# Prompt attention scores in two rounded passes, and the samples' block scores sample by sample

## The reference

```python
s_c = jnp.einsum('btgrd,bngd->bgrtn', q, kc).astype(jnp.float32) * scale - slopes[:, :, None, None] * dist_c
p_c = masked_softmax(s_c, dist_c >= 0, (-1,))
o_cmp = jnp.einsum('bgrtn,bngd->btgrd', p_c, vc.astype(jnp.float32))
...
ss = jnp.einsum('qgrd,gqkld->grqkl', qb, kg).astype(jnp.float32) * scale - slopes[:, :, None, None, None] * dist[:, None]
pp = masked_softmax(ss, (dist >= 0)[:, None], (-2, -1))
...
ss = jnp.einsum('bqgrd,bkgd->bgrqk', qb, kv[:, :, 0]).astype(jnp.float32) * scale - slopes[:, :, None, None] * dist.astype(jnp.float32)
o = gates[..., 0:1] * o_cmp + gates[..., 1:2] * o_slc + gates[..., 2:3] * o_win
```

## Time and profile before

| | us |
|---|---|
| median of 3 runs | 4044.45 |
| runs | 4039.71 to 4048.02 |
| the profiled execution's own time | 4041.04 |
| its span in the profile | 4039.4 |
| the four rounds of the prompt's attention, first product with block keys to last transposes | 230.0 to 647.3 |
| fetch of the samples' blocks | 1018 to 1109 |
| TensorE busy over the span | 3489.2 (86%) |
| mean granted TensorE clock | 0.914 of full |

### The profile page before, as it was taken

The page is one execution under the profiler, slowest core; times in us unless marked ns, Lnnn a source line. Parts: engine busy times, 40 slices in busy tenths (PEclk is TensorE's granted clock), DMA queues, the critical chain, the costliest instruction groups (busy, mean ns, idle before and its releaser), DMA issues. The chain is left out here.

```text
span 4039.4 us, 64008 instructions
## 1 busy us (share of the span) xinstructions
PE 3489.2 (86%) x22287; PEld 3282.6 (81%) x22287; DVE 1353.9 (34%) x2028; ACT 1344.8 (33%) x2211; POOL 1483.8 (37%) x964
## 2 busy tenths in 40 slices
PE   5988887898088888799999998798997899999997
PEld 4966665898058777799999997788886799999997
DVE  3034442001003445443343332043345344343342
ACT  2134442000003443244344442233323244344442
POOL 2300001332403222246666664122222256666663
PEclk8978887899569999899999999899999899999998
DMA  1400001785200001134444443101111134444443
GB/s 71 129 17 0 0 0 48 258 266 164 78 11 32 32 32 58 59 99 139 137 138 149 144 151 106 48 28 39 51 38 54 58 114 133 138 140 133 143 137 124
DMA packets 158153, 372.99 MB, mean 92 GB/s; under 512 B 22410, under 2 KB 78026, under 8 KB 156316
## 3 DMA queue, kind: packets, MB, share of 16 engines
q1 hardware_dynamic: 116828, 310.96, 23.9%
q10 hardware_dynamic: 29440, 32.78, 2.5%
q0 software_dynamic: 11776, 27.80, 2.1%
HBM read 352.76 MB, written 22.89 MB: 93 GB/s over the span
## 5 line engine op out<-in xcount | busy, mean ns | idle before, releaser
L493 POOL TENSOR_TENSOR back_WL<-back_RAW,back_WH 128x1024 fp32r<-128x1024 f32 (+1 forms) x408 | 956.1, 2350 | 679.3 <-ACT back_WH L594 678.2
L532 PE MATMUL PS<-back_TH,back_WH 128*128 128x344 f32 x2112 | 676.9, 321 | 13.9 <-DVE back_TL L703 13.9
L532 PE MATMUL PS<-back_TL,back_WH 128*128 128x344 f32 x2112 | 674.7, 319 | 0.0
L532 PE MATMUL PS<-back_TH,back_WL 128*128 128x344 f32 x2112 | 674.4, 319 | 0.0
L594 ACT ACTIVATE back_WH<-back_RAW 128x1024 fp32r<-128x1024 f32 (+1 forms) x408 | 421.6, 1033 | 523.2 <-DMA back_RAW<-in_w 350.7
L532 PEld LDWEIGHTS PS<-back_TH,back_WH 128*128 128x128 f32 x2112 | 397.9, 188 | 15.6 <-issue 15.6
L532 PEld LDWEIGHTS PS<-back_TL,back_WH 128*128 128x128 f32 x2112 | 398.0, 188 | 0.0
L532 PEld LDWEIGHTS PS<-back_TH,back_WL 128*128 128x128 f32 x2112 | 397.8, 188 | 0.0
L741 DVE TENSOR_TENSOR back_HL<-back_TMP,back_HH 128x344 f32 x132 | 323.1, 2447 | 126.5 <-ACT back_HH L607 126.5
L1076 PE MATMUL PS<-layer_XH,layer_WH 128*128 128x344 f32 x960 | 325.9, 339 | 32.8 <-POOL layer_WL L1026 28.5
L532 PE MATMUL PS<-back_HH,back_WH 128*128 128x344 f32 x1056 | 338.4, 320 | 0.0
(11 more groups left out here) (365 smaller groups left out, 6079.3 us busy)
## 6 DMA issues: line engine op xcount, KB each, us to landing
back_RAW<-in_w SPq DMA_DIRECT2D x360, 512.0 KB, 3.3
layer_AR<-in_cmp SPq DMA_DIRECT2D x192, 128.0 KB, 4.3
layer_AR<-in_cmp POOLq DMA_DIRECT2D x192, 128.0 KB, 4.1
back_RAW<-in_w SPq DMA_DIRECT2D x48, 384.0 KB, 3.1
layer_AR<-in_cmp ACTq DMA_DIRECT2D x128, 128.0 KB, 4.1
layer_WR<-in_w_even SPq DMA_DIRECT2D x54, 256.0 KB, 2.8
layer_WR<-in_w_odd SPq DMA_DIRECT2D x50, 256.0 KB, 2.9
XT<-in_xT SPq DMA_DIRECT2D x4, 1032.0 KB, 7.8
```

The source lines that it names most:

```text
L493: pool.tensor_tensor(lo, raw, hi.bitcast(F32), ALU.subtract).then_inc(wl_ready, 1)
L532: mm = pe.matmul(m.PS[:, bank, 0:CH], wgt[:, t % RING, w], tok[:, k0 + k], start=(k0 + k + n == 0), stop=(last and n == 2 and k == kt - 1))
```

## The change

**Prompt scores.** The queries are now split: `m.QS` has, for group g, the query rounded to fp32r in g's own 64 rows (ScalarE, as before) and the remainder, rounded too, in the other 64 rows that were zero (VectorE, a new subtraction in each round for each group). The keys are doubled over both row halves and rounded (`m.KHD`, one tensor for each kind and group, in the place of tiles that are no longer needed), and their remainders stand in `m.KL`. One scores product becomes two fp32r products into the same PSUM region: `QS` (128 rows) by `KHD` (high query and low query by high key), then the 64 rows of the high query by `KL`. The block keys likewise become `KCH` and `KCL`, both over 128 rows. The splits are made at the start of the stage: kind 0's rounding on ScalarE (four copies of 64x1024) and its remainders on VectorE, kind 1's both on GpSimd (four products by one and two subtractions, 64x1024 each), the block keys' on VectorE. The large memset of `m.QP` goes.

**Samples.** The fetch loops are unrolled over the eight samples, each sample has its own two semaphores, and TensorE goes through the products sample by sample: it waits for that sample's blocks, and does for each group the first row half and then the second.

```diff
@@ attention_memory
-    m.QP = carve(m.AR, r, (G, SEQ))
+    m.QS = nc.alloc_sbuf_tensor_at("att_QS", [P, G, SEQ], F32R, offset=m.at_ar + 4 * r)
+    m.KHD = [[nc.alloc_sbuf_tensor_at(f"att_KHD{kind}{g}", [P, SEQ], F32R, offset=m.at_ar + 4 * TOK * tile)
+              for g, tile in enumerate(tiles)] for kind, tiles in enumerate(((TKC, TVC), (TVS, TVW)))]
+    m.KL = [nc.alloc_sbuf_tensor_at(f"att_KL{kind}", [P, SEQ], F32R, offset=m.at_ar + 4 * TOK * tile)
+            for kind, tile in enumerate((TKS, TKW))]
...
@@ attention
-        zeroed = m.dve.n + 2
+        zeroed = m.dve.n + 1
+        halves = [slice(g * DH, (g + 1) * DH) for g in range(G)]
...
+        @block.gpsimd
+        def _(pool):
+            for g in range(G):
+                for half in (halves[g], halves[1 - g]):
+                    pool.tensor_tensor(m.KHD[1][g][half], NT[halves[g], TKW, 0:SEQ],
+                                       m.ones[halves[g], 0:1].to_broadcast([DH, SEQ]), ALU.mult).then_inc(kx_ready, 1)
+            pool.wait_ge(kx_ready, 4 + ONE)
+            for half, high in zip(halves, m.KHD[1]):
+                pool.tensor_tensor(m.KL[1][half], NT[half, TKW, 0:SEQ], high[half].bitcast(F32), ALU.subtract)\
+                    .then_inc(kx_ready, 1)
...
+                    if s == 0:
+                        pe.wait_ge(kl_ready, 2 + ONE)
+                    elif s == QT:
+                        pe.wait_ge(kx_ready, 6 + ONE)
+                    half = halves[g]
                     for a in range(k0, k1, 512):
                         b = min(a + 512, k1)
-                        mm = pe.matmul(sbank(s)[:, a - k0:b - k0], m.QP[:, g, i * P:(i + 1) * P],
-                                       NT[:, TKS if kind == 0 else TKW, a:b], start=True, stop=True)
+                        pe.matmul(sbank(s)[:, a - k0:b - k0], m.QS[:, g, i * P:(i + 1) * P], m.KHD[kind][g][:, a:b],
+                                  start=True, stop=False)
+                        mm = pe.matmul(sbank(s)[:, a - k0:b - k0], m.QS[half, g, i * P:(i + 1) * P],
+                                       m.KL[kind][half, a:b], start=False, stop=True)
...
-                pe.wait_ge(q_ready, (r + 1) * 2 + ONE)
+                pe.wait_ge(kc_ready, 8 + ONE)
+                pe.wait_ge(ql_ready, (r + 1) * 2 + ONE)
...
-                        mm = pe.matmul(m.PS[:, 7, c0:c0 + PBLK], m.QP[:, g, i * P:(i + 1) * P], m.KCT,
-                                       start=True, stop=True)
+                        pe.matmul(m.PS[:, 7, c0:c0 + PBLK], m.QS[:, g, i * P:(i + 1) * P], m.KCH[:, g],
+                                  start=True, stop=False)
+                        mm = pe.matmul(m.PS[:, 7, c0:c0 + PBLK], m.QS[:, g, i * P:(i + 1) * P], m.KCL[:, g],
+                                       start=False, stop=True)
...
         @block.scalar
         def _(act):
+            for g in range(G):
+                act.activation(m.KHD[0][g][halves[g]], NT[halves[g], TKS, 0:SEQ], ACT.Copy).then_inc(kh_ready, 1)
+            for g in range(G):
+                act.activation(m.KHD[0][g][halves[1 - g]], NT[halves[g], TKS, 0:SEQ], ACT.Copy).then_inc(kh_ready, 1)
...
             t = m.dve
-            t.up(dve.memset(m.QP, 0.0))
             t.up(dve.memset(m.PC, 0.0))
+            for g in range(G):
+                for half in (halves[g], halves[1 - g]):
+                    dve.tensor_copy(m.KCH[half, g], m.KCT[halves[g]]).then_inc(kc_ready, 1)
...
+            dve.wait_ge(kh_ready, 4 + ONE)
+            for half, high in zip(halves, m.KHD[0]):
+                dve.tensor_tensor(m.KL[0][half], NT[half, TKS, 0:SEQ], high[half].bitcast(F32), ALU.subtract)\
+                   .then_inc(kl_ready, 1)
...
+                    dve.wait_ge(q_ready, r * 2 + g + 1 + ONE)
+                    dve.tensor_tensor(m.QS[halves[1 - g], g:g + 1], NT[halves[g], ds(r, 1), 0:SEQ],
+                                      m.QS[halves[g], g:g + 1].bitcast(F32), ALU.subtract).then_inc(ql_ready, 1)
@@ sample_select
-            with eng.Fori(0, NB) as b:
+            for b in range(NB):
...
-            pe.wait_ge(blocks_in, 20 * NB * 16)
-            pe.wait_ge(pool_in, 10 * NB * 16)
             pe.wait_ge(idx_ready, 2)
-            for half in range(2):
-                rows = slice(half * DH, (half + 1) * DH)
-                for n in range(NBG16):
+            for n in range(NBG16):
+                if n % G == 0:
+                    pe.wait_ge(blocks_in[n // G], 20 * 16)
+                    pe.wait_ge(pool_in[n // G], 10 * 16)
+                for half in range(2):
+                    rows = slice(half * DH, (half + 1) * DH)
                     mm = pe.matmul(m.PS[0:ROWS, 2 + half, :].rearrange("p (a b) -> p a b", b=BLK),
```

More of the change, by code:

```diff
@@ L1509, in _, with attention_memory @@
             closing(HEADS - 1, False)
-def attention_memory(m):
+def attention_memory(nc, m):
     W = m.WR
@@ L1527, in attention_memory @@
     m.HC = carve(m.AR, r + 4352, (2, G * PBLK), 0, DH)
-    m.QP = carve(m.AR, r, (G, SEQ))
+    m.QS = nc.alloc_sbuf_tensor_at("att_QS", [P, G, SEQ], F32R, offset=m.at_ar + 4 * r)
[3 more added lines that the diff above has]
+            for kind, tile in enumerate((TKS, TKW))]
+    at_kc = m.at_ar + 4 * (r + 6144)
+    m.KCH = nc.alloc_sbuf_tensor_at("att_KCH", [P, G, PBLK], F32R, offset=at_kc)
+    m.KCL = nc.alloc_sbuf_tensor_at("att_KCL", [P, G, PBLK], F32R, offset=at_kc + 4 * G * PBLK)
     m.AS = carve(m.LC, 0, (G, SEQ))
@@ L1664, in attention @@
         q_ready = sem("q_ready")
+        ql_ready = sem("ql_ready")
+        kh_ready, kl_ready = sem("kh_ready"), sem("kl_ready")
+        kx_ready, kc_ready = sem("kx_ready"), sem("kc_ready")
         bias_ready = sem("bias_ready")
@@ L1759, in _ @@
         def _(act):
+            for g in range(G):
+                act.activation(m.KHD[0][g][halves[g]], NT[halves[g], TKS, 0:SEQ], ACT.Copy).then_inc(kh_ready, 1)
+            for g in range(G):
+                act.activation(m.KHD[0][g][halves[1 - g]], NT[halves[g], TKS, 0:SEQ], ACT.Copy).then_inc(kh_ready, 1)
             with act.Fori(0, R) as r:
-                act.wait_ge(m.dve.sem, zeroed)
                 act.wait_ge(qk_ready, r * NS + ONE)
                 for g in range(G):
-                    half = slice(g * DH, (g + 1) * DH)
-                    act.activation(m.QP[half, g:g + 1], NT[half, ds(r, 1), 0:SEQ], ACT.Copy).then_inc(q_ready, 1)
+                    act.activation(m.QS[halves[g], g:g + 1], NT[halves[g], ds(r, 1), 0:SEQ], ACT.Copy)\
+                       .then_inc(q_ready, 1)
                 act.wait_ge(cp_step, r * 9 + 3 + ONE)
@@ L1798, in _ @@
             t = m.dve
-            t.up(dve.memset(m.QP, 0.0))
             t.up(dve.memset(m.PC, 0.0))
+            for g in range(G):
+                for half in (halves[g], halves[1 - g]):
+                    dve.tensor_copy(m.KCH[half, g], m.KCT[halves[g]]).then_inc(kc_ready, 1)
+            dve.wait_ge(kc_ready, 4 + ONE)
+            for g in range(G):
+                for half in (halves[g], halves[1 - g]):
+                    dve.tensor_tensor(m.KCL[half, g], m.KCT[halves[g]], m.KCH[halves[g], g].bitcast(F32), ALU.subtract)\
+                       .then_inc(kc_ready, 1)
+            dve.wait_ge(kh_ready, 4 + ONE)
+            for half, high in zip(halves, m.KHD[0]):
+                dve.tensor_tensor(m.KL[0][half], NT[half, TKS, 0:SEQ], high[half].bitcast(F32), ALU.subtract)\
+                   .then_inc(kl_ready, 1)
             dve.wait_ge(t.sem, zeroed)
@@ L2236, in sample_select @@
         idx_ready = sem("idx_ready")
-        blocks_in = sem("blocks_in")
-        pool_in = sem("pool_in")
+        blocks_in = [sem(f"blocks_in{b}") for b in range(NB)]
+        pool_in = [sem(f"pool_in{b}") for b in range(NB)]
         ss_ready, ss_neg, se_ready = sem("ss_ready"), sem("ss_neg"), sem("se_ready")
@@ L2248, in fetch @@
             eng.wait_ge(idx_ready, 1)
-            with eng.Fori(0, NB) as b:
+            for b in range(NB):
                 for n in range(0, len(slots), 4):
                     some = slots[n:n + 4]
-                    rows = [eng.value_load(m.IDX[0:1, ds(b * (G * TOPK) + slot, 1)]) for slot in some]
+                    rows = [eng.value_load(m.IDX[0:1, b * (G * TOPK) + slot:b * (G * TOPK) + slot + 1]) for slot in some]
                     for slot, row in zip(some, rows):
@@ L2255, in fetch @@
                         half = slice(s % 2 * DH, s % 2 * DH + DH)
-                        eng.dma_start(m.KVG[half, ds(b, 1), g, s // 2], d["slc"][ds(row, 1), g]
+                        eng.dma_start(m.KVG[half, b:b + 1, g, s // 2], d["slc"][ds(row, 1), g]
                                       .rearrange("n p c -> p n c"))\
-                            .then_inc(pool_in if eng is nc.gpsimd else blocks_in, 16)
+                            .then_inc((pool_in if eng is nc.gpsimd else blocks_in)[b], 16)
         @block.sync
@@ L2427, in program @@
             with mixer_memory(nc, m, "layer0"):
```

(2 more changed lines are left out.)

## The result

The changed kernel takes 4192.92 us (median of 4 runs, 4181.94 to 4248.02) against 4045.13 of the kernel before: a ratio of 1.0358, 95% interval 1.0319 to 1.0397. The ratio leaves out the run of 4248.02, which lies 1.6% above the fastest. The change makes the kernel slower by 3.6%, inside the forecast's range and on its side, but 83 us under its number.

A forecast was written before the change was run, and what follows sets the result against it. TensorE bounds the prompt attention's steps, and the samples' fetch and products are exposed. From 4041.04 us, 248 + 11.5 + 18 - 36 - 7 = +234.5 gave 4275.5, rounded to 4276 us; range 4090 to 4320.

The forecast's parts named there:

- rival 1: Prompt attention: the clock rises to 2.4 GHz in part of the stage; 4155 us, range 4070 to 4230, chance 0.12.
- c: Prompt attention: TensorE's clock stays at 1.2 GHz for the whole stage; +62 us a round, +248 for four.
- rival 3: Score pairs: free mode change, 3971 us, chance 0.07; above about 0.10 us a change costs over a third of the saving.
- a: Prompt scores: two fp32r passes stream in half the float32 time, saving 14.1 us a round at 2.4 GHz.
- b: Scores: 96 changes between 128 and 64 rows a round, 0.20 us at full clock (19.2 us), 0.30 at 1.2 GHz.
- d: Head of a round: TensorE waits for VectorE's biases and query subtractions; +3.8 us in three rounds, +11.5.
- e: Start of the attention stage: VectorE's splits, slowed beside GpSimd's work, delay TensorE; +18 us.
- f: Samples' stage: seven samples' products hide behind the fetch and the row halves run together; -36 us.
- g: Samples' fetch: unrolled loops need no register instruction for the block number; -7 us, bounds -9 and +9.
- Rival 2: Prompt attention: the clock rises as today; 4040 us, unchanged, range 4025 to 4055, chance 0.10.

The follow-up runs named there:

- grouped: The changed kernel with both 128-row products first, then both 64-row ones, in steps with two key pieces; 4180.98 us, ratio 1.0323.
- full_rows: The changed kernel with the second pass of each pair over all 128 rows, against both groups' key remainders; 3999.86 us, ratio 0.9889.
- full_heads: full_rows with both query remainders before group 1's biases and GpSimd's six operations after round 0's small softmax; 3982.08 us, ratio 0.9834.
- twice: The changed kernel with the first product of every pair issued twice; 4224.26 us, ratio 1.0413.
- narrow: The changed kernel with both passes over the high query's 64 rows, low query by high key left out; 4188.75 us, ratio 1.0326.
- full_changes: full_rows with a 64-row product of 128 columns put ahead of every pair, which overwrites it; 4100.16 us, ratio 1.0153.

## Why the prediction was right or wrong

- **The case.** The forecast was that the clock stays at 1.2 GHz for the whole stage, with 0.71. What came is rival 1, with 0.12: the clock rose in parts, at the place that the rival named, the widest causal steps. The rival gave 4155 and a range of 4070 to 4230; 4192.92 lies in it. That is luck: the forecast's own case, 4235 to 4310, misses, and the range holds the result by rival 1's share of it. The failed step is in c: "I take it that the clock stays there for the whole stage." It rose in three rounds of four and was full for 111 of 582 us. The rows that c rested on showed stretches of narrow products in which the clock stayed down, while the new steps keep transposes and values over 128 rows. The kernel before had a row for that: behind the 24 us of L1611 at 1.2 GHz the clock rose at 218.7, in the middle of 16 transposes over 128 rows (L1616), as it rises behind the eight of the widest causal step here.
- **The sum.** +234.5 forecast, +140.9 between the profiled executions: the rounds came out 94.5 under, the samples 5.4 under and the start 2.1 under, and 8.4 came from stages for which the forecast had nothing. The bounds of its own case don't follow from the terms named for them, which give 4226 to 4295. Nor does rival 3's "a third": 0.10 us at 96 changes is 9.6 of the 14.1 us saved, two thirds.
- **a and b, the passes and the changes.** Right. At full clock the pair of 512 columns takes 0.84 us, of which the columns need 2 x 0.213, and two changes the rest: 0.20 a change, as b has it. That is no more than float32's 4 x 0.213, but the pair of 128 columns takes 0.52 against 0.213. "I take 0.30" at 1.2 GHz measured 0.30 (grouped). That widening the 64-row products turns the loss into a gain (full_rows) shows them as the cause. By b and d at the clock of before, the rounds would have lost only 4 x 5.1 + 3 x 3.9 = 32 of their 165 us, an estimate; the other 133 are the lower clock. The Trainium skill ("TensorEngine Tiling (Array Packing)", Key Properties) says that changing the tiling mode drains TensorE. The trace agrees that there is a delay, a 64-row product starting 0.41 us after one whose columns need 0.213 (497.45 to 497.86), but no run divides the delay between a drain and the weight load.
- **c, the size.** A whole round at 1.2 GHz took 166.35 us, 60.9 more than before; c and d made it 65.8. The step of five tiles was put at 5.5 and took 5.35. Over four rounds: 259.5 forecast (c and three heads), 165.0 measured; 20 of the difference lie in that price and 75 in the clock.
- **d, the head of a round.** 3.8 forecast, 8.3 - 4.4 = 3.9 measured, and full_heads took 2.4 of it away (8.29 to 5.91 us of idle time).
- **e, the start.** 18 forecast, 15.9 measured. About 8 came from VectorE's own list and about 8 from GpSimd beside it, as full_heads shows. In detail it went otherwise: the key remainders began at 229.93, not 238.5, since no small operation waited for a whole one of GpSimd's, and took 3.27 us each, not the 1.23 reckoned.
- **f, the samples' products.** 36 forecast, 39.6 - 3.7 = 35.9 measured, the row halves together.
- **g, the unrolled fetch.** "I take -7", with a bound at -9; 12 measured. The step counted only the number's own instruction. The address computation and issue of every DMA on SyncE got cheaper too.
- **Rivals 2 and 3.** Rival 2's arithmetic (4040 with the clock of before) wasn't put to the test by any run. Rival 3 (the change is free) is refuted by the 0.20 at full clock. The Trainium skill's rule of keeping TensorE busy to get past half rate ("TensorE: Matmul & The Clock Gate", Why this matters for your kernels) doesn't decide this case: 60.00 of 60 busy microseconds at 1.2 GHz in twice speak against taking it as enough.

## What to carry to other kernels

Here a product over half the rows between products over all of them cost two changes, 0.20 us each at 2.4 GHz and 0.30 at 1.2. If the other half's operand is harmless, let the product run over all rows. Where a stage lives from the full clock, a cheaper instruction mix can lose it, and the engine's busy share does not tell. Look for stretches of the trace that resemble each part of the new mix, and forecast a partial rise as the likeliest case when they disagree. Price a change at equal clock first, step by step, since there the sums hold to a few per cent.

## What was not expected of the hardware

The same program differs by 53 us from run to run (narrow, 4160.68 to 4213.43, at mean clocks of 0.858 to 0.876), by 66 in the changed kernel and by 41 in full_changes. The versions whose profile shows an early rise in every round stay within 6 to 12 us (full_rows, full_heads). VectorE's tiny operations are longer beside GpSimd's too: a 64x16 subtraction takes 0.96 us there and 0.17 alone. And a DMA whose place is a loop variable costs SyncE 32 ns more in address computation than one at a fixed place, besides the register instruction for its number.
